# A decoder step on one core: warming TensorE on ones, loading the prompt's rows ahead of W_in, and queries inside the z tiles

## The reference

```
z = x @ w_in                      # 1024 -> 3072 columns: [q | k | v | B | C | h]
sample attention:  gate = q . mean of each block's keys, top 3 of 8 blocks and the own token
                   s = q.k / 8 - slope * distance; softmax; p @ v
conv mixer:        B * dwconv3_causal(C * h)
x1 = LayerNorm(alpha * x + concat(attn, conv) @ w_out)
y  = LayerNorm(alpha * x1 + (silu(a) * g) @ w_ffn_down),  a, g = dwconv3_causal(x1 @ w_ffn_up)
```

## Time and profile before

| what | value |
|---|---|
| median of 3 runs | 437.27 us (436.94 to 438.08) |
| the profiled execution | 437.8 us |
| its span in the profile | 436.0 us |
| busy: PE, DVE, ACT, POOL | 412.7, 294.7, 181.4, 110.8 us |
| moved by DMA | 124.6 MB, mean 286 GB/s |

### The profile page before, as it was taken

One profiled execution on the slowest core, in us unless ns is written; L12 is line 12 of the kernel. 1 busy time (PEld: TensorE's weight loads), 2 busy tenths in 40 slices (PEclk: granted clock), 3 DMA queues, 4 the chain that ended last, 5 costly groups with the idle time before them and its releaser, 6 DMA issues.

```text
span 436.0 us, 8237 instructions
## 1 busy us (share of the span) xinstructions
PE 412.7 (95%) x2903; PEld 339.2 (78%) x2903; DVE 294.7 (68%) x382; ACT 181.4 (42%) x694; POOL 110.8 (25%) x133
## 2 busy tenths in 40 slices
PE   4999999999999998999999989999999999999990
PEld 4588887876876774765653479999999999999990
DVE  0498999999799976954541275666776776534437
ACT  1587569644469133112110243554455555233201
POOL 1005334995255152200000717122211220000002
PEclk9999999999999999999999999999999999999997
DMA  8999999899999999999999953665556766676002
GB/s 313 397 359 407 405 407 393 316 404 409 409 359 327 338 404 405 406 405 404 402 405 398 318 196 98 194 191 162 158 169 191 213 181 186 183 211 206 3 2 99
DMA packets 109515, 124.60 MB, mean 286 GB/s; under 512 B 5903, under 2 KB 67048, under 8 KB 109466
## 3 DMA queue, kind: packets, MB, share of 16 engines
q1 hardware_dynamic: 101138, 107.30, 70.2%
q10 hardware_dynamic: 8336, 16.78, 10.2%
HBM read 121.65 MB, written 2.61 MB: 285 GB/s over the span
## 4 chain that ended last, share of the span: by engine, by line
PE 64%; DVE 18%; DMA 5%; issue 5%; SPq 4%; POOL 2%; ACT 1%; DVEq 0%; POOLq 0%; ACTq 0%
PE ps L1821 12%; PE ps L1822 11%; PE ps L1823 11%; PE ps L1714 8%; PE ps L1608 6%; DVE qk L939 6%; DVE T L949 5%; PE ps L1437 4%; PE ps L1632 4%; PE ps L1634 3%; PE ps L1384 3%; SPq L360 2%; DMA wring<-in_cache_v 2%; DMA KV<-in_cache_k 2%; POOL x1l L612 1%
## 5 line engine op out<-in xcount | busy, mean ns | idle before, releaser
L1188 DVE TENSOR_TENSOR wlo<-KV,whi 128x2048 fp32r<-128x2048 f32 (+1 forms) x24 | 61.7, 2571 | 57.5 <-ACT whi L838 29.3
L1437 PE MATMUL ps<-xT,wring 128*128 128x264 f32 x384 | 89.6, 388 | 0.1
L1437 PEld LDWEIGHTS ps<-xT,wring 128*128 128x128 f32 x384 | 71.6, 190 | 13.6 <-issue 1.7
L1821 PE MATMUL ps<-x1h,whi 128*128 128x264 f32 x256 | 73.7, 288 | 0.2
L1822 PE MATMUL ps<-x1l,whi 128*128 128x264 f32 x256 | 72.7, 284 | 0.0
L1823 PE MATMUL ps<-x1h,wlo 128*128 128x264 f32 x256 | 72.6, 284 | 0.0
L939 DVE TENSOR_TENSOR qk<-KV,qk 128x1536 f32<-128x1536 f32 (+1 forms) x32 | 67.0, 2097 | 6.6 <-DMA KV<-in_cache_k 2.7
L669 ACT ACTIVATE qk<-qk 128x64 f32<-128x64 f32 x216 | 51.9, 245 | 29.1 <-POOL qk L560 23.1
L949 DVE TENSOR_REDUCE T<-qk 128x24 f32<-128x1536 f32 (+1 forms) x32 | 58.4, 1827 | 0.0
L1821 PE MATMUL ps<-fh,whi 128*128 128x264 f32 x176 | 50.4, 286 | 0.1
L1822 PE MATMUL ps<-fl,whi 128*128 128x264 f32 x176 | 50.0, 284 | 0.0
(11 more groups left out here) (215 smaller groups left out, 574.0 us busy)
## 6 DMA issues: line engine op xcount, KB each, us to landing
KV<-in_cache_k SPq DMA_DIRECT2D x128, 256.0 KB, 6.2
KV<-in_w_ffn_up SPq DMA_DIRECT2D x32, 512.0 KB, 4.7
KV<-in_cache_v SPq DMA_DIRECT2D x60, 256.0 KB, 7.3
wring<-in_cache_v SPq DMA_DIRECT2D x56, 256.0 KB, 6.4
KV<-in_w_ffn_down SPq DMA_DIRECT2D x8, 1408.0 KB, 6.3
wring<-in_w_in ACTq DMA_DIRECT2D x5, 2048.0 KB, 14.0
zbuf<-in_cache_v SPq DMA_DIRECT2D x12, 256.0 KB, 5.3
zbuf<-in_w_ffn_up SPq DMA_DIRECT2D x3, 1024.0 KB, 10.2
```

The lines of the kernel that those rows point to most:

```text
L1188: nc.vector.tensor_tensor(wlo[s][:, 0:n], w2[s][:, 0:n], whi[s][:, 0:n], ALU.subtract).then_inc(s_lo, 1)
L1437: ins = nc.tensor.matmul(ps[:, z_bank(n), 0:R], tile[k], xT[:, k, :], start=k == 0, stop=k == KT - 1)
L1821: nc.tensor.matmul(out, wh[k], xh[k], start=k == 0, stop=False)
```

## The change

Four things change.

1. `WARM` is 11 in place of 14, the matmuls read `ones` in place of `ident`, and they stand ahead of the waits for `ident` and `srows`. POOL sets `ones` before it sets `xsP`.
2. The prompt's rows are issued by ACT, as its first transfer. Chunk 0 of W_in is issued by SP, behind `sel`, once `ident` has landed. The keys stand behind it.
3. Six of the eight `x_transposes` stand ahead of the query product (four before), the last two behind it; ACT copies all eight ahead of `load_win(1)`.
4. `query(b)` stands in the middle of z tile b on PE (four matmuls, the query, four matmuls). On ACT its copy stands ahead of the copy of z tile b. The stack's transposes and copies stand behind z tile 5, not 3. `load_win(2)` and `load_win(3)` stand ahead of `sum_products(3)` and `sum_products(7)`.

```diff
-WARM = 14
+WARM = 11
...
-            sp.dma_start(rows, x_prompt[0].rearrange("(r p) d -> p r d", p=P)).then_inc(s_x, 16)
+            sp.wait_ge(s_id, 16)
+            sp.dma_start(wring[:, 0, :].rearrange("p (k n) -> p k n", k=KT),
+                         win[:, :, Z_ORDER[0] * DA:(Z_ORDER[0] + 1) * DA]).then_inc(s_win[0], 16)
             sp.wait_ge(s_pt, 16)
...
+            nc.gpsimd.memset(ones, 1.0).then_inc(s_ones, 1)
             nc.gpsimd.memset(xsP, 0.0).then_inc(s_pad, 1)
-            nc.gpsimd.memset(ones, 1.0).then_inc(s_ones, 1)
...
-            load_win(0)
+            act.dma_start(rows, x_prompt[0].rearrange("(r p) d -> p r d", p=P)).then_inc(s_x, 16)
...
-            for k in range(6):
+            for k in range(KT):
                 x_copy(k)
-            query(0)
-            x_copy(6)
-            x_copy(7)
             load_win(1)
-            query(1)
-            sum_products(0)
-            for j in range(1, 4):
-                z_tile(j - 1)
-                query(2 * j)
-                query(2 * j + 1)
+            for j in range(3):
+                query(j)
+                z_tile(j)
                 sum_products(j)
+            query(3)
             z_tile(3)
             load_win(2)
+            sum_products(3)
+            for j in range(4, 6):
+                query(j)
+                z_tile(j)
+                sum_products(j)
...
-            for j in range(4, 8):
-                sum_products(j)
-                z_tile(j)
+            query(6)
+            z_tile(6)
+            sum_products(6)
+            query(7)
+            z_tile(7)
             load_win(3)
+            sum_products(7)
...
+            pe.wait_ge(s_ones, 1)
+            for i in range(WARM):
+                nc.tensor.matmul(ps[:, 5, 0:P], ones, ones, start=True, stop=True)
             pe.wait_ge(s_id, 16)
             pe.wait_ge(s_xs, 16)
...
-            for i in range(WARM):
-                nc.tensor.matmul(ps[:, 5, 0:P], ident, ident, start=True, stop=True)
...
-            for k in range(4):
+            for k in range(6):
                 x_transposes(k)
             pe.wait_ge(s_xsP, 1)
             pe.wait_ge(s_win[0], 16)
...
-            for k in range(4, 6):
+            for k in range(6, KT):
                 x_transposes(k)
-            pe.wait_ge(s_qs, 3)
 
             def query(b):
-                if b >= 2:
+                if b == 0:
+                    pe.wait_ge(s_qs, 3)
+                elif b >= 2:
                     pe.wait_ge(s_qb, b - 1)
...
-            query(0)
-            x_transposes(6)
-            x_transposes(7)
-            query(1)
-            for n in range(3):
-                z_tile(n)
-                query(2 * n + 2)
-                query(2 * n + 3)
-            z_tile(3)
+            for n in range(6):
+                z_tile(n, lambda: query(n))
             pe.wait_ge(s_stack, 64)
...
-            z_tile(4)
-            z_tile(5)
-            z_tile(6)
-            z_tile(7)
+            z_tile(6, lambda: query(6))
+            z_tile(7, lambda: query(7))
```

## The result

| | before | after |
|---|---|---|
| time, median of 4 runs | 437.29 us (436.94 to 438.08) | 441.23 us (440.75 to 441.48) |
| ratio | | 1.0076, 95% interval 1.0061 to 1.0092 |
| span of the profiled execution | 436.0 us | 439.5 us |

What follows compares the result with a forecast made beforehand. DMA, then a chain of waits through DVE's multiplies, was taken as the bound, with key arrival deciding. Idle DMA + 0.7 and chunk 2 ahead of group 6 + 1.8 gave + 2.5 us: median 439.8 us, range 436.2 to 442.0.

Steps and rivals of the forecast that it cites:

- Step 1: Start of the transfers: prompt's rows land at about 5.9 us, chunk 0 at T = 11.8.
- idle DMA of 0.7 us: DMA idle before chunk 0's first data, making everything behind chunk 0 0.7 us later (0 to 1.4).
- The case of the Trainium skill: DMA queues take turns by packets of several descriptors, delaying chunk 0: T = 12.9, result 1.1 us above the forecast.
- Step 2: TensorE: first z tile 3.5 us earlier at 15.3, but multiply 0 at 18.2 against 17.98, DVE losing 0.2 us.
- Step 3: Keys of group 4: same bytes ahead in another order, landing at 34.5, so DVE is + 0.7 us at multiply 4.
- Step 4: Chunk 2, issued at 30.9, takes turns from group 6's keys: DVE + 2.5 us in all from multiply 6 on.
- + 1.8: The sum's term for chunk 2's data going ahead of group 6's keys: 1.8 us.
- What is moved besides costs nothing: Stack copies two z tiles later, with POOL's work on them ending some 4 us later, cost no time.
- the term that was to decide: Chunk 2 among the keys ahead of group 6, put at + 1.8 us in the sum.
- The keys are hardly late: Rival: chunk 2 gets later turns or keys over half; + 0.7 to + 1.3 us, 438.0; chance 0.18.
- faster: Rival: group 4's keys land by 32.4, multiply 4 follows without that wait, DVE 1.6 us early, 435.7; chance 0.15.
- TensorE cools: Rival: PE slows in its wait of about 2 us before chunk 0 lands; + 0.7 to + 1.3, 438.3; chance 0.07.

Runs made afterwards that it cites:

- e10: After plus eight filler matmuls ahead of the query product, chunk 1 issued behind query 0's copy and chunk 2 behind z tile 4; ratio 1.0088, 441.81 us.
- e11: After's start with eight filler matmuls, before's order of queries, z tiles and stack, chunk 1 behind the sums of group 0; ratio 1.0029, 439.44 us.
- e9: After plus eight filler matmuls on ones, keeping PE busy ahead of the query product's waits; ratio 1.0082, 441.40 us.
- e5: Before with chunk 1 of W_in issued behind the fourth copy of the prompt's blocks, not the eighth; ratio 1.0006.
- e2: After with chunk 2 of W_in issued later, behind z tile 4; ratio 1.0077, 441.63 us.
- e3: After with before's start (transfers, warming, four blocks ahead of the product), keeping the new query order, ACT order and stack place; ratio 1.0062, 440.89 us.
- e8: After's start (transfers, warming on ones, six blocks ahead of the product) with before's order of queries, z tiles, stack and ACT; ratio 1.0013.
- e12: After's start with eight filler matmuls, before's order, chunk 1 behind the eighth block's copy; ratio 1.0023, 439.02 us.
- e1: After with chunk 1 of W_in issued later, behind query 0's copy; ratio 1.0049.
- e4: After with the four stack transfers issued by SP ahead of its wait for the page table; ratio 1.0088.
- e7: After with the stack's transfers and the constants issued by POOL, not SP; ratio 1.0065.

## Why the prediction was right in its side and short in its size

**Step 1** held: chunk 0 had landed when the product started at 11.56 (forecast 11.8). The idle DMA of 0.7 us was not there: in 5:6 the engines moved 317 GB/s at a share of 1.05, where the us around it have 400: some 0.2 us. The case of the Trainium skill (DMA: Bandwidth & Descriptors, "Queues, rings and completion order"), by which T would have been 12.9, did not come either: T was 11.5, from the issue at 3.35 and 8.1 us to landing.

**Step 2** held: product 11.56 (11.8), z tile 0 at 15.11 (15.3), multiply 0 at 18.02 (18.2), and that the half tile takes back what the earlier product gave. e10 and e11 give its price, 1.75 us.

**Step 3 is the one that failed.** It put the issue of SP's own transfers at nothing. It said that "the same bytes stand ahead of them now, in another order", so that group 4 lands at 34.5. The bytes were the same, but the keys were issued later, and meanwhile the DMA engines moved 218 GB/s (28:32), where before had 375. Chunk 1 was issued 3.67 us earlier, SP's issue of `w_ffn_conv` took 5.40 us, group 4 was issued 4.1 us later, and multiply 4 stood at 37.42. The prediction knew chunk 1's new time ("about 15.2") and costed only small packets with it, up to 1.0 us. How the stall follows chunk 1, over the kernels in which SP issues the stack at 17 us:

| chunk 1 issued | issue of `w_ffn_conv` | group 4 issued | kernel |
|---|---|---|---|
| 13.44 | 4.93 | 28.27 | e5 |
| 14.58 | 5.40 | 28.85 | after |
| 14.73 | 4.90 | 28.00 | e9 |
| 15.88 | 2.77 | 27.27 | e2 |
| 17.83 | 1.28 | 26.14 | e3 |
| 18.25 | 0.53 | 24.77 | before |
| 19.08 | 1.01 | 23.80 | e8 |
| 21.37 | 0.91 | 23.56 | e12 |
| 21.69 | 0.89 | 24.77 (behind multiply 0) | e1 |
| 22.24 | 0.62 | 25.32 (behind multiply 0) | e10 |
| 24.05 | 0.75 | 23.57 | e11 |

The issue starts between 17.26 and 17.64 in all of them, so in the last six chunk 1 had no part in it, and 0.53 to 1.01 us is what it takes by itself. That an earlier chunk 1 makes it long is shown by e5, one edit in before; why the issue is held is not shown.

**Step 4** was right in its mechanism, and mis-sized: chunk 2 was issued at 30.55 (30.9) and its packets stood among the keys', but it met groups 4 and 5, not 5 and 6, because these were late themselves. The term "+ 1.8" measured about 3: e9 and e5 issue group 4 within 0.3 us of each other, at 28.00 and 28.27, chunk 2 at 30.70 and 34.72, and are 3.77 and 0.95 us late at multiply 7, which is 2.8 us; after against e2 gives 3.3, with a part of the stall in it. "Multiply 6 near 44.9" with a wait was wrong: it stood at 46.77 without one. The idle term, + 0.7, is not seen. The stall without chunk 2 is about 1.0 (e5 and e2), and the 4.4 us at multiply 7 stand where the sum had 2.5.

**"What is moved besides costs nothing"** was wrong by 0.4 us in after: beside POOL's work on the stack multiply 7 takes 2.90 us; in before multiply 5 stood beside it and took 2.46, and the others 2.29. In e2 such meetings of DVE and POOL cost 0.7 us at multiply 7 and 3.1 more later, of which three multiplies clear of POOL gave 1.1 back: more than the term that was to decide.

**The end.** "Every later stage 2.5 later" held in kind: the lateness is 5.0 us from multiply 8 to 25 and at 30, and penx stands at 104.18, not 101.7. The span grew by 3.5 only. The stretch from multiply 30 to the end took 262.2 us in before and 260.7 in after; over the fourteen profiles it lies between 260.7 and 262.2 with no tie to the edits, so I read this as the spread of the stretch, and left its cause open. That the time came out within 1.4 us of the forecast is in part luck: a stall of 1 us, 1.2 us more for chunk 2 and 0.4 at multiply 7 were missing in the sum, 0.7 of idle DMA was in it for nothing, and 1.5 us went in the last stretch. And the term that was to decide does not decide the time: with chunk 2 later, in e2, the ratio is the same.

**Rivals.** "The keys are hardly late" and "faster" fell with multiply 4. "TensorE cools" did not happen in the profile of after, in its wait of 1.51 us; it did in e1, in a wait of 2.33 us, and in e4 and e8 already in the last transposes ahead of the wait, while the keys or the chunks, not the product, set DVE's place in e8. What no rival named is the case of e2, e3, e4 and e10: the keys are in time or nearly, and the kernel is as slow by other ways, the later multiply 0, instructions of DVE beside POOL, and in e3 the wait for PE. So in e2 to e4 and e10 a repair of the keys brought nothing back; e1, with its two groups of runs, leaves this open. Only the kernels with the old order came within 0.3% of before, and none of the twelve was measurably faster.

## What to carry to other kernels

Before a transfer is moved forward, look at what the other issuing engine does in the next microseconds: here one of its issues was held for up to 5 us, and what is issued behind it was late although no byte was added. In after it was this one issue; in before the constants were issued behind chunk 1's issue, at 19.3 to 24.6, and took 0.3 to 1.5 us each. When a loss is repaired in one stage and the time stays, follow the lateness from instruction to instruction: in e2 it came back by DVE instructions that had lengthened, and the wait that stood out, 1.09 us for PE, was paid back within three multiplies. A head start of TensorE for which nobody waits can turn into a wait and a lower clock; ask of each gained microsecond which instruction will stand and wait with it. And take the new order and the new start apart before judging either: here the new order of queries, z tiles and copies cost about 2.4 us, and the new start brought nothing measurable.

## What the runs showed of the hardware

An issue on SP's queue took from 0.53 to 5.40 us for the same transfer, and in e5 the only edit was when 2 MB were issued in ACT's queue (table above). It is not bound to a place: moved forward in e4 it took 3.59 us. Issued by POOL, at 15.30 in e7, it took 0.69 us.

DVE instructions took longer beside POOL's. The multiply of 128x2048 took 2.29 us, and 2.46 to 3.05 where it started behind an instruction of POOL's work on the stack (2.46 in before's multiply 5, 2.90 in after's multiply 7, 3.05 in e7's). Where it started first it kept its 2.29 us: before's multiply 6 at 42.37, POOL's cast of `ident` at 42.38. Short ones took about as long as POOL's instruction beside them: in e2 `ownT` 1.32 us beside 1.27, where before had 0.22.

TensorE's warming at the very start gave no steady pace. Of the ten profiled executions with the new start, three had the product at 1.92 us (after, e7, e9). In e1, e4 and e8 it took 3.64 us, at a granted clock of 0.50, the 1.2 GHz level. In e1 the engine had waited 2.33 us just before; in e4 and e8 the clock fell while it still did the last blocks of transposes (granted 0.68 and 0.87 in 8:10) and before a wait of 1.4 and 1.7 us. In e2, e10, e11 and e12 it took 2.76 to 2.94 us with a granted clock of 1.00 throughout. There the engine was at half pace from the beginning: the filler's sixteen matmuls took 3.78 us in e10 and 2.05 in e9. So the granted clock of a window did not tell the pace; the duration of a known matmul did. All four profiles with the old start had 1.92 us.

```profile
11.85 3.78 PE L1414 MATMUL ps<-ones 128*128 128x128 f32 x16
```

And the clock fell in after behind a wait of 4.83 us at 47 us for ACT's copy of a query; the next z tile took 6.59 us in place of 3.83. It cost the end nothing that the trace shows, as DVE did not wait for PE there:

```profile
52.01 0.26 PE L1390 MATMUL ps<-ident,lnr 16*128 16x16 f32 x1 [4.83 <-ACT qk L659]
52.20 6.59 PE L1445 MATMUL ps<-xT,wring 128*128 128x264 f32 x16
```
